# Dilated attention in a two-part transformer block on one Trainium2 core: another order of the work between the projections

## The reference, cut to what matters

```python
def dilated_attention(h, w_in, w_o, rel_bias):
    proj = (h @ w_in).reshape(B, S, N_GROUPS, 3, DIL_HEADS, DIL_HEAD_DIM)
    for g, (window, dilation) in enumerate(DIL_GROUPS):        # (128, 1), (512, 4), (2048, 16)
        o, lse = strided_window_attention(proj[:, :, g, 0], proj[:, :, g, 1], proj[:, :, g, 2],
            dilation, window // dilation, rel_bias[:, g * DIL_HEADS:(g + 1) * DIL_HEADS])
        ...
    alpha = jax.nn.softmax(jnp.stack(lses, axis=0), axis=0)
    o = jnp.sum(alpha[..., None] * jnp.stack(outs, axis=0).astype(jnp.float32), axis=0)
    return o.astype(h.dtype).reshape(B, S, DIL_WIDTH) @ w_o

# inside strided_window_attention: s = q k / 8 + bias[bucket(distance)], masked outside the window
#   lse = logsumexp(s);  p = exp(s - lse);  o = p v
```

## Time and profile before

| | us |
|---|---|
| median of 3 runs | 3871.89 |
| lowest and highest | 3866.84, 3872.97 |
| the profiled execution's own time | 3879.0 |
| its span | 3876.9 |
| PE busy | 3619.1 (93%) |
| DVE busy | 2017.1 (52%) |
| ACT busy | 1333.8 (34%) |
| chain that ended last: PE, DVE, ACT, DMA | 81%, 11%, 4%, 2% |

### The profile page before, as it was taken

The page is one execution under the profiler, slowest core; times in us unless marked ns, Lnnn a source line. Parts: engine busy times, 40 slices in busy tenths (PEclk is TensorE's granted clock), DMA queues, the critical chain, the costliest instruction groups (busy, mean ns, idle before and its releaser), DMA issues.

```text
span 3876.9 us, 40995 instructions
## 1 busy us (share of the span) xinstructions
PE 3619.1 (93%) x16372; PEld 2876.8 (74%) x16372; DVE 2017.1 (52%) x3608; ACT 1333.8 (34%) x2291; POOL 128.0 (3%) x126
## 2 busy tenths in 40 slices
PE   5899999899999999988999999999999889869998
PEld 4647888666888788866678887888777777757886
DVE  7856756676766654466763236324633222345234
ACT  3563323343423332334442233223322232233222
POOL 2330000000000000001100000000000000000000
PEclk9999999989999999999999999999999999979999
DMA  6214554413555455320022222222222222122221
GB/s 244 98 44 160 203 191 180 151 56 110 195 185 195 174 195 195 114 74 33 22 66 99 99 95 80 99 94 97 86 73 63 78 63 62 45 63 87 98 93 65
DMA packets 155466, 429.06 MB, mean 111 GB/s; under 512 B 45467, under 2 KB 50523, under 8 KB 155276
## 3 DMA queue, kind: packets, MB, share of 16 engines
q1 hardware_dynamic: 155276, 426.45, 31.5%
HBM read 423.98 MB, written 2.40 MB: 110 GB/s over the span
## 4 chain that ended last, share of the span: by engine, by line
PE 81%; DVE 11%; ACT 4%; DMA 2%; issue 1%; SPq 1%; POOL 0%; ACTq 0%; DVEq 0%; POOLq 0%
PE ps L412 23%; PE ps L414 23%; PE ps L413 23%; ACT SD L1306 1%; PE ps L786 1%; PE ps L711 1%; DMA lse<-small 1%; DMA small<-lse 1%; PE ps L456 1%; PE ps L449 1%; DVE TT L1483 1%; DVE HL L1468 1%; DVE wlo L1416 1%; PE ps L751 1%; DVE X L1569 1%
## 5 line engine op out<-in xcount | busy, mean ns | idle before, releaser
L412 PE MATMUL ps<-HH,whi 128*128 128x512 f32 x3168 | 1264.9, 399 | 58.9 <-DVE HL L1468 28.1
L413 PE MATMUL ps<-HL,whi 128*128 128x512 f32 x3168 | 1245.9, 393 | 0.0
L414 PE MATMUL ps<-HH,wlo 128*128 128x512 f32 x3168 | 1245.5, 393 | 0.0
L1416 DVE TENSOR_TENSOR wlo<-wraw,whi 128x1024 fp32r<-128x1024 f32 x526 | 643.8, 1224 | 702.5 <-ACT whi L891 702.3
L891 ACT ACTIVATE whi<-wraw 128x1024 fp32r<-128x1024 f32 x548 | 576.1, 1053 | 652.7 <-PE ps L414 640.3
L412 PEld LDWEIGHTS ps<-HH,whi 128*128 128x128 f32 x3168 | 603.0, 190 | 216.7 <-issue 63.3
L414 PEld LDWEIGHTS ps<-HH,wlo 128*128 128x128 f32 x3168 | 602.5, 190 | 128.8
L413 PEld LDWEIGHTS ps<-HL,whi 128*128 128x128 f32 x3168 | 603.4, 190 | 127.2 <-issue 4.6
L1404 DVE CUSTOM_DVE_ANT_0 mraw<-mraw,CB 128x1024 f32<-128x1024 f32 x224 | 282.6, 1263 | 0.6 <-DMA mraw<-mst 0.6
L1602 DVE TENSOR_TENSOR TT<-TT,ps 128x512 f32<-128x512 f32 x116 | 79.7, 687 | 217.1 <-PE ps L414 187.8
L412 PE MATMUL ps<-PHf,whi 128*128 128x512 f32 x352 | 136.9, 389 | 0.0
(11 more groups left out here) (325 smaller groups left out, 3931.3 us busy)
## 6 DMA issues: line engine op xcount, KB each, us to landing
wraw<-wst SPq DMA_DIRECT2D x548, 512.0 KB, 3.4
mraw<-mst SPq DMA_DIRECT2D x224, 512.0 KB, 3.4
MR<-mst SPq DMA_DIRECT2D x16, 512.0 KB, 13.6
X<-xt SPq DMA_DIRECT2D x8, 256.0 KB, 5.1
BB<-bvec SPq DMA_DIRECT2D x8, 256.0 KB, 3.7
TT<-lse SPq DMA_DIRECT2D x16, 128.0 KB, 3.0
out<-X SPq DMA_DIRECT2D x8, 256.0 KB, 2.0
CB<-crow SPq DMA_DIRECT2D x2, 512.0 KB, 4.5
```

Source lines behind the costliest of these rows:

```text
L412: e.matmul(o[key], wh, sh(k), start=k == 0, stop=False)
L413: e.matmul(o[key], wh, sl(k), start=False, stop=False)
L414: ins = e.matmul(o[key], wl, sh(k), start=False, stop=k == nk - 1)
L1416: e.tensor_tensor(wlo[:, x % SPLIT, :], wraw[:, x % RAW, :], whi[:, x % SPLIT, :].bitcast(F32), ALU.subtract).then_inc(*wlo_made.up(x))
```

## The change

The instructions and their number stay the same; their order changes on PE and DVE. ACT's and SP's programs are not touched.

- The transposes of the values (`turn_values`, was inside `head_proj`) stand one projection later: those of groups 0 and 1 after projections n = 3 and n = 6, those of group 2 after n = 0 of the next pair. DVE's copy (`values_in`) moves with them.
- The transposes of the probabilities (`turn_probs`) are split off from `values`. Those of head 0 stay in step 6, and their `values` moves to step 7; those of head 1 stay in step 7, after `values` of head 0, and their `values` moves to step 8. The row of the sums stays in step 7 and now stands ahead of `values` of head 1.
- `column_of` moves from the end of step 4 into the projection of step 5, after the second of its eight tiles. DVE's `column_in` moves from step 4 to 5, `spread_probs` from 6 and 7 to 7 and 8.
- `invert` moves from step 8 to step 1 of the next pair, `finish` from step 1 to step 3 there.

```diff
@@ TensorE
-                def head_proj(c, n):
+                def head_proj(c, n, between=None):
                     if c or n >= 4:
-                        proj([("dl", c, n)], 8, hh, hl, ready)
-                    g = n // 3
-                    if n % 3 == 2:
-                        o = take(("vt", c, g), main[0])
...
+                        proj([("dl", c, n)], 8, hh, hl, ready, between)
+
+                def turn_values(c, g):
+                    o = take(("vt", c, g), main[0])
+                    lane.wait_ge(a_mix, ("vt", c, g))
...
-                def values(c, hh_):
-                    vn, sd = VN[c % 2], SD[hh_]
+                def turn_probs(c, hh_):
+                    sd = SD[hh_]
...
+                def values(c, hh_):
+                    vn = VN[c % 2]
...
-                    elif step == 4:
-                        column_of(c)
                     elif step == 6:
+                        turn_probs(c, 0)
+                    elif step == 7:
                         take(("od", c), ob)
                         values(c, 0)
-                    elif step == 7:
+                        turn_probs(c, 1)
+                        row_of(("sr", c), cs[:, 0, :, :], a_mix, ("ex", c, 1))
+                    elif step == 8:
                         values(c, 1)
-                        row_of(("sr", c), cs[:, 0, :, :], a_mix, ("ex", c, 1))
...
                         if c < 7:
-                            head_proj(c + 1, step)
+                            head_proj(c + 1, step, (lambda k: column_of(c) if k == 1 else None) if step == 5 else None)
+                            if step in (3, 6):
+                                turn_values(c + 1, step // 3 - 1)
+                        elif step == 5:
+                            column_of(c)
+                        if step == 0:
+                            turn_values(c, 2)
                         attend(c, step)
@@ VectorE
...
                             head_proj(c + 1, step)
+                            if step in (3, 6):
+                                values_in(c + 1, step // 3 - 1)
                         elif step >= 2:
                             keep(step - 2)
+                        if step == 0:
+                            values_in(c, 2)
...
-                        elif step == 4:
+                        elif step == 5:
                             column_in(c)
-                        elif step == 6:
+                        elif step == 7:
                             spread_probs(c, 0)
-                        elif step == 7:
-                            spread_probs(c, 1)
                             row_out(("sr", c), 2, sum_out)
                         elif step == 8:
-                            invert(c)
+                            spread_probs(c, 1)
                         if step == 1 and c:
+                            invert(c - 1)
+                        elif step == 3 and c:
                             finish(c - 1)
+                invert(7)
                 finish(7)
                 keep(7)
```

More of the change, by code:

```diff
@@ L730, in dilated @@
                 proj([("dl", 0, n) for n in range(4)], 8, hh, hl, ready)
-                def head_proj(c, n):
+                def head_proj(c, n, between=None):
                     if c or n >= 4:
-                        proj([("dl", c, n)], 8, hh, hl, ready)
-                    g = n // 3
-                    if n % 3 == 2:
-                        o = take(("vt", c, g), main[0])
[L738 to L741, removed]
+                        proj([("dl", c, n)], 8, hh, hl, ready, between)
+                def turn_values(c, g):
+                    o = take(("vt", c, g), main[0])
+                    lane.wait_ge(a_mix, ("vt", c, g))
+                    for j in range(4):
+                        ins = e.transpose(o[:, 128 * j:128 * j + 128], VT[:, g, 128 * j:128 * j + 128], C["ident"][:])
+                    ins.then_inc(*mm_done.up(("vt", c, g)))
                 def logits(c, hh_):
@@ L830, in dilated @@
                     head_proj(0, n)
+                    if n in (3, 6):
+                        turn_values(0, n // 3 - 1)
                 for c in range(8):
@@ L1971, in head_proj, with values_in @@
                         freed[key] = ((v_mix, ("dk", c, g)),)
[L1972 to L1979, removed]
+                def values_in(c, g):
+                    key = ("vt", c, g)
+                    lane.wait_ge(mm_done, key)
+                    if c >= 2:
+                        lane.wait_ge(mm_done, ("od", c - 2, 1))
+                    e.tensor_copy(VN[c % 2][:, 4 * g:4 * g + 4, :], bank(key).rearrange("p (j f) -> p j f", j=4)).then_inc(
+                        *v_mix.up(("vn", c, g)))
+                    freed[key] = ((v_mix, ("vn", c, g)),)
                 def biased(c, hh_):
@@ L2055, in dilated @@
                     head_proj(0, n)
+                    if n in (3, 6):
+                        values_in(0, n // 3 - 1)
                 for c in range(8):
```

## The result

The changed kernel takes 3814.47 us (median of 4 runs, 3814.20 to 3821.20), the kernel before 3871.36 in the same comparison (3866.84 to 3872.97). The ratio is 0.9859, with a 95% interval of 0.9842 to 0.9876: 56.9 us faster. The forecast was 3802 in a range of 3785 to 3834; the direction and the range held, and the gain was 57 where 69 had been worked out. The profiled execution took 3821.2 (span 3819.1) against 3879.0 before.

A forecast was written before the change was run, and what follows sets the result against it. PE sets the pace, losing 12.0 us per cycle to waits and slow clock. Gain 12.0 - 1.3 - 0.9 - 0.3 = 9.5, over seven cycles 66.5, plus 1.9 and tail 1.0: 3871.9 - 69.4 = 3802, range 3785 to 3834.

The forecast's parts named there:

- full-speed cycle: One pair's nine steps on PE without the listed losses: 69.15 us, against a mean cycle of 81.17.
- Value transposes: L740's waits for ACT's VT, 2.8 us per cycle, go at no cost when moved behind the next projection.
- Probabilities: Step 6, L776 to L786 and the products after: losses of 4.54 and 1.66 us per cycle go.
- `RB`: Head 0's L798 in step 7 newly waits 1.3 us per cycle for DVE's spread_probs, bounds 0 to 3.0.
- `column_of`: L811's wait for the maxima falls from 1.65 to 0.9 us per cycle, bounds 0 to 3.2.
- Clock: Slow PE clock after the new idle of 1.3 us costs 0.3 us per cycle.
- rival 2: The RB wait pulls the clock down in each cycle, some 2.5 us per cycle: 3820 us; chance 0.20.
- Tail: Pair 7: row of the sums 3.42 us earlier, inverses(6) ahead of maxima(7) costs 2.4; net gain 1.0.
- Rival 1: No new wait: RB and maxima in time, clock stays up; 17.5 us better, 3785; chance 0.13.
- Rival 3: Burst of loads delays the maxima: 3.2 us idle, 2.7 slow clock, 5 per cycle: 3837; chance 0.12.
- Rival 4: SP, held until invert, starves the weights; 21 us late would give 3886; chance 0.05 with others like it.

The follow-up runs named there:

- e4: Changed kernel with invert back in step 8 and spread_probs of head 0 ahead of the weight split; 3789.29 us.
- e1: Kernel before with only the value transposes and DVE's copy of them a projection later; 3843.16 us.
- e3: Changed kernel with DVE's spread_probs of head 0 ahead of the weight split and the copy of k; 3805.10 us.
- e2: Changed kernel with DVE's invert back in step 8; 3796.88 us.
- e5: Changed kernel with only SP's order altered: inverses(c - 1) at n = 5, just ahead of maxima, instead of n = 2; 3803.56 us.
- e8: Kernel before with only invert moved to step 1 and finish to step 3 of the next pair; 3883.34 us.
- e9: Kernel before with the value transposes a projection later, invert in step 1 and finish in step 3; 3867.31 us.

## Why the prediction was right or wrong

Inside the stage the sum said 69.4 and the traces show 53.2: the six cycles gave 41.4 where 57.0 had been worked out, pair 0 gave 9.4 (11.4 worked out, after taking off 3.42 by which a `values` moved across the mark), the tail 2.4 (1.0). The profiled executions as a whole differ by 57.8, with 4.4 from an earlier start of the stage that is none of the change's doing; whether the medians, 56.9 apart, hold as much of that is not known.

- **The full-speed cycle** of 69.15: right. e4 runs at 69.19 with PE never idle.
- **Value transposes**, 2.8 gone at no cost: right in the changed kernel, no idle before L740 of the cycles. e1 brings 4.3, since less idle also means less slow clock, and since pair 3's slow cycle is not in that run.
- **Probabilities**, 4.54 and 1.66 gone, no wait at L776 or at the products: right.
- **`RB`**, "L798 waits 1.3": right, 1.32 in the timeline and 1.5 from start to start. The chain behind it (split, copy of k, `spread_probs`) is what e3 takes apart, and e3 gives it back.
- **`column_of`: this is the step that failed**, by the size of one term. The sentence was: "so about 1 us is added". Its own figures do not give the 1: loads of 4.8 that start 2 us ahead of writes issued over 2.6 outlast them by 0.2. Nor do the terms beside it give the 0.9: 0.7 for DVE's copy and 1 for SP, less 0.3 of cover, make 1.4. SP's wait for the small writes rose by 2.6, from 8.3 / 6 to 24.0 / 6. I had counted only by how much the loads outlast the issuing of the small writes; but the read that follows needs all of them complete. It went out 7.4 us after the first write, some 3 us after the DMA share had fallen to nothing. Idle at L814 is 2.18 in the mean instead of 0.9, which lies within my bounds of 0 to 3.2 but far above the value taken. e2 and e5 show the cause, by taking the loads away from ahead of the writes in two ways. The rule of the Trainium skill on the order within a ring (DMA: Bandwidth & Descriptors, Queues, rings and completion order) was the better guide than the row I had. It has a DMA engine take the descriptors of one ring in order, and the trace of the changed kernel agrees: only 33 packets under 512 bytes went while 1.38 MB of loads moved, and 615 in the 1.2 us behind them. e5, with the same transfers and no burst ahead of the writes, agrees too.
- **Clock**, 0.3: it was 1.25. It follows from the last point: the idle that I took to be 0.9 was up to 2.79, and after it PE ran slow in four of six cycles. Without that idle (e2, e5) the clock is 1.00, with the `RB` wait still there. So rival 2, which had the `RB` wait pull the clock down, is refuted for this kernel by the same two runs.
- **Tail**: the two terms were near, and the sum is off by one that was left out. From the transposes of head 1 to the output projection 20.1 us became 17.0, so 3.1 where 3.42 had been counted. `inverses(6)` ahead of `maxima(7)` cost 2.7 instead of 2.4. The other 2.0 of the gain lie ahead of the row of the maxima, where the sum had nothing: the value transposes' wait of 0.94 is gone there as well, and the logits of head 1 met less of the slow clock.
- **Rivals.** Rival 1 (no new wait) did not come; e4 had to be built for it. Rival 3, the burst, came true in part: with 2.18 of idle and 1.25 of clock its 5 us per cycle beyond the forecast were 2.2 (1.3 of idle, 0.95 of clock). Rival 4, the starved weights, did not come: no wait for weights in any version, though SP stands 23.7 us at the inverses in the mean.

What I got wrong beside the size is that I priced the parts as a sum. The same move of `invert` costs 1.2 or 3.4 us per cycle, and what differs is how near another part brings the maxima to the loads (e8, e9). The 1.2 is one execution's mean over unlike cycles, so the two prices are surely different but not sharp.

## What to carry to other kernels

When a small step is moved that a DMA-issuing queue waits for, look at what stands behind that wait in the queue: transfers that used to leave one by one leave together once it is over, and a small round trip issued right behind them lands late. Price such a round trip by its completion, not by the share of the burst that its issue overlaps. Piece the full-speed cycle together from the places where the limiting engine stands still; it tells what all repairs together can give, and here putting `invert` back and one further small move gave 25 us more.

## What the runs showed of the hardware

- **Order and completion behind a burst.** In pair 2 of the changed kernel the small writes' packets go only when the three loads issued ahead of them have moved (33 packets under 512 bytes in 3.8 us, then 615 in 1.2 us). In e2, with no burst ahead, they go while the writes are still being issued, 440 of them in the 2.6 us from the first write:
```profile
DMA packets 448, 0.01 MB, mean 4 GB/s; under 512 B 440, under 2 KB 448, under 8 KB 448
```
In the changed kernel the DMA share is about 1 until some 2983.6 and 0.00 from 2984.2, and the read that waits for the writes is issued only at 2986.58. The trace has the counts of their semaphore come in one after the other, all but the first from 2983.49 to 2986.56; in e2 they come from 2975.52 to 2978.72, beside the issuing, and the wait is 1.0. So what the burst put off is nearly the whole of the completion, some 3 us. Why the counts take so long stays open; no run here separates it.
- **Small idles and the clock.** After idle of 1.73, 2.29, 2.73 and 2.79 us at L814 the granted clock of the following projection fell, after 2.22 and 1.33 it did not. In e9 it did not even after 2.60, 2.92 and 3.32. Two of the changed kernel's, L814 and the next value transposes, from the timeline:
```profile
3069.21 0.38 PE L814 MATMUL ps<-c_ident,rows 8*128 8x8 f32 x2 [2.22 <-DMA small<-lse]
3079.22 0.38 PE L740 MATMUL ps<-c_ident,VT 128*128 128x128 f32 x2
...
3288.60 0.38 PE L814 MATMUL ps<-c_ident,rows 8*128 8x8 f32 x2 [2.29 <-DMA small<-lse]
3300.18 0.49 PE L740 MATMUL ps<-c_ident,VT 128*128 128x128 f32 x3
```
The same work takes 10.01 and 11.58 us after nearly the same idle. So the length of idle alone does not decide, and the idle of 1.73 us, with 1.57 lost to slow matmuls behind it (again 11.58), cost nearly twice its own length. The forecast's rows showed idle of 4.46 followed by slow products, 0.91 followed by none, and nothing between. The trace of the kernel before has more: at L811 half speed came after 1.75 and 3.21 of idle, and not after 1.62.
